# Loads and position products at the start of a hybrid S5 / pool / conformer step: small loads first, raw parameters turned in pairs, one product per position row

## The reference

```python
lam_bar = jnp.exp(lam * dt)
b_bar = ((lam_bar - 1.0) / lam)[..., None] * bmat
mod = jax.nn.silu(c) @ ada_w + ada_b
xs = x_sample + _grid_pos_embed(rows, GRID_W, D_MODEL)
h = _rmsnorm(x, norm1_g) * (1.0 + sc1) + sh1
z = h @ w_in
```

## Time and profile before

| | us |
|---|---|
| median of 3 runs | 1314.56 |
| lowest and highest run | 1313.19, 1315.68 |
| the profiled execution's own time | 1311.89 |
| its span, first to last instruction | 1310.0 |
| TensorE busy (share of the span) | 1219.5 (93%) |
| VectorE busy | 857.4 (65%) |
| ScalarE busy | 510.2 (39%) |
| POOL busy | 521.7 (40%) |

### The profile page before, as it was taken

The page is one execution under the profiler, slowest core; times in us unless marked ns, Lnnn a source line. Parts: engine busy times, 40 slices in busy tenths (PEclk is TensorE's granted clock), DMA queues, the critical chain, the costliest instruction groups (busy, mean ns, idle before and its releaser), DMA issues.

```text
span 1310.0 us, 21433 instructions
## 1 busy us (share of the span) xinstructions
PE 1219.5 (93%) x7574; PEld 1072.3 (82%) x7574; DVE 857.4 (65%) x1336; ACT 510.2 (39%) x911; POOL 521.7 (40%) x362
## 2 busy tenths in 40 slices
PE   3888899996699999899999999999999999999996
PEld 2478898786446888899999999999889999999995
DVE  2647959989944337667767666766855555555558
ACT  1464451126245547533333433433432333333223
POOL 0179425554343003455444445444533333333330
PEclk9889999997799999999999999999999999999998
DMA  8833345389872333766666576566677778777781
GB/s 273 313 110 120 114 140 177 102 109 229 270 290 97 104 121 102 252 226 229 219 208 211 189 256 224 213 219 220 237 232 250 240 260 277 255 249 264 242 279 73
DMA packets 189569, 268.52 MB, mean 205 GB/s; under 512 B 14030, under 2 KB 108536, under 8 KB 186824
## 3 DMA queue, kind: packets, MB, share of 16 engines
q1 hardware_dynamic: 187952, 263.00, 61.8%
q0 software_dynamic: 1280, 4.72, 0.9%
q10 hardware_dynamic: 280, 0.09, 0.0%
HBM read 186.49 MB, written 81.26 MB: 204 GB/s over the span
## 4 chain that ended last, share of the span: by engine, by line
PE 79%; DVE 8%; ACT 3%; DMA 3%; issue 3%; POOL 2%; SPq 1%; ACTq 0%; DVEq 0%; POOLq 0%
PE banks L891 22%; PE banks L893 22%; PE banks L892 22%; PE banks L1163 3%; PE banks L927 1%; PE banks L1042 1%; PE banks L976 1%; DMA dn<-in_ssm_d 1%; POOL sst L820 1%; PE banks L1059 1%; PE banks L1065 1%; PE banks L962 1%; ACT nts L1700 1%; DVE dsel L1959 1%; PE banks L935 1%
## 5 line engine op out<-in xcount | busy, mean ns | idle before, releaser
L843 POOL TENSOR_TENSOR raw13r<-raw13s,w13h 128x512 fp32r<-128x512 f32 x110 | 155.4, 1421 | 467.0 <-ACT w13h L1652 421.8
L892 PE MATMUL banks<-ntr,w13h 128*128 128x256 f32 (+1 forms) x1144 | 336.8, 294 | 0.0
L891 PE MATMUL banks<-ntr,w13h 128*128 128x256 f32 (+1 forms) x968 | 283.0, 292 | 3.4 <-POOL raw13r L843 2.2
L892 PEld LDWEIGHTS banks<-ntr,w13h 128*128 128x128 f32 x1144 | 215.9, 189 | 0.9
L891 PEld LDWEIGHTS banks<-ntr,w13h 128*128 128x128 f32 x968 | 183.0, 189 | 5.6 <-issue 2.5
L891 PE MATMUL banks<-f2h,f_hi 128*128 128x512 f32 x396 | 156.7, 396 | 0.4 <-DVE acc L2360 0.4
L893 PE MATMUL banks<-f2h,f_lo 128*128 128x512 f32 x396 | 156.2, 395 | 0.0
L892 PE MATMUL banks<-f2l,f_hi 128*128 128x512 f32 x396 | 156.2, 395 | 0.0
L893 PE MATMUL banks<-ntr,raw13r 128*128 128x256 f32 (+1 forms) x528 | 153.9, 291 | 0.0
L2226 DVE TENSOR_TENSOR acc<-acc,banks 128x512 f32<-128x512 f32 x170 | 112.9, 684 | 38.9 <-PE banks L893 30.8
L847 POOL TENSOR_TENSOR f2l<-f2s,f2h 128x1024 fp32r<-128x1024 f32 x44 | 106.3, 2437 | 34.7 <-ACT f2h L1656 34.7
(11 more groups left out here) (323 smaller groups left out, 2536.5 us busy)
## 6 DMA issues: line engine op xcount, KB each, us to landing
raw13s<-in_ffn_w SPq DMA_DIRECT2D x66, 512.0 KB, 4.5
parts<-w13h SPq DMA_DIRECT2D x110, 256.0 KB, 2.5
w13h<-parts SPq DMA_DIRECT2D x110, 256.0 KB, 2.8
f2s<-in_ffn_w SPq DMA_DIRECT2D x44, 512.0 KB, 4.2
ad<-in_ada_w SPq DMA_DIRECT2D x20, 1024.0 KB, 9.1
parts<-wsumr SPq DMA_DIRECT2D x66, 256.0 KB, 2.6
wsumr<-parts SPq DMA_DIRECT2D x55, 256.0 KB, 4.9
parts<-raw13r SPq DMA_DIRECT2D x44, 256.0 KB, 2.9
```

What stands on the lines that cost most here:

```text
L843: nc.gpsimd.tensor_tensor(w13_low(x, f), w13_low(x, f, F32), w13h[x][:, :, :].bitcast(F32), ALU.subtract).then_inc(sem("w13_lo"), 1)
L891: nc.tensor.matmul(out, hi_w, hi_x, start=start, stop=False)
L892: nc.tensor.matmul(out, hi_w, lo_x, start=False, stop=False)
```

## The change

Seven edits, all before the first input projection:

- SP issues the two state rows, the taps and ssm_d, which ACT issued, behind the lambda rows, ahead of all large loads; ACT issues the nine groups of parameter rows alone.
- The four raw tensors lie on four quarters (32 partitions each) of one buffer, in a place of their own behind the eight modulation tiles.
- SP no longer waits for the raw turns; x tiles and modulation tiles 0 to 3 alternate.
- `raws_turn` turns two tensors at once: 16 transposes of 64 partitions for B, 32 products of 64 partitions for C. It signals twice instead of four times, and the readers' views go over two banks.
- POOL copies the identity into two selectors, `col_sel` (64 x 128) and `row_sel` (16 x 8 x 128).
- `pos_columns` and `pos_row` are one product each, of 128 output partitions, with these selectors.
- Position rows 4 and 5 go between the modulation tiles, rows 6 and 7 behind the eighth turn of x.

```diff
-    raw = [at(f"raw{i}", [32, 2 * HD * NS], O_NT + 40960 + i * 8192) for i in range(4)]
+    raw = at("raw", [4 * Q, 2 * HD * NS], O_NT + KT * 8192)
+    row_sel = at("row_sel", [16, 8, P], O_W2 + 4096)
+    col_sel = at("col_sel", [GRID_W, P], O_W2 + 8192)
...
-        for i, name in enumerate(("ssm_lam_re", "ssm_lam_im")):
+        for i, name in enumerate(("ssm_lam_re", "ssm_lam_im", "state_ssm_re", "state_ssm_im")):
             sp.dma_start(rlam[:, i, :], dview(A[name], 0, [[P, Q], [1, P]])).then_inc(sem("vectors_in"), 16)
-        ada_in(0)
-        ada_in(1)
+        sp.dma_start(rtap[:, :], dview(A["conv_dw_w"], 0, [[P, 2 * TAPS], [1, P]])).then_inc(sem("vectors_in"), 16)
+        sp.dma_start(dn[:, :], dview(A["ssm_d"], 0, [[32, NPAIR], [1, 32]])).then_inc(sem("vectors_in"), 16)
         for i, name in enumerate(("ssm_b_re", "ssm_b_im", "ssm_c_re", "ssm_c_im")):
-            sp.dma_start(raw[i][:, :], dview(A[name], 0, [[2048, Q], [1, 2048]])).then_inc(sem("raws_in"), 16)
+            sp.dma_start(raw[Q * i:Q * i + Q, :], dview(A[name], 0, [[2048, Q], [1, 2048]])).then_inc(sem("raws_in"), 16)
         sp.dma_start(pos_c[:, :], A["pos_cols"]).then_inc(sem("pos_in"), 16)
         sp.dma_start(pos_r[:, :], A["pos_rows"]).then_inc(sem("pos_in"), 16)
-        x_in(0)
-        ada_in(2)
-        x_in(1)
-        ada_in(3)
-        x_in(2)
-        x_in(3)
+        for n in range(4):
+            x_in(n)
+            ada_in(n)
         ada_in(4)
         ada_bias(0)
-        sp.wait_ge(sem("raws_turned"), 3)
         for n in range(5, KT):
             ada_in(n)
...
+        pool.wait_ge(sem("ident"), 1)
+        nc.gpsimd.tensor_copy(view(col_sel, 0, [[GRID_W, 2], [1, GRID_W]], 0, GRID_W),
+                              view(ident, 0, [[0, 2], [1, GRID_W]], 0, GRID_W)).then_inc(sem("ident"), 1)
+        nc.gpsimd.tensor_copy(view(row_sel, 0, [[GRID_W, 16], [1, GRID_W]], 0, 16),
+                              view(ident, 0, [[1, 16], [0, GRID_W]], 0, 16)).then_inc(sem("ident"), 1)
...
-            for i in range(4):
-                for h in range(HD):
-                    if i < 2:
-                        last = tr(B[i][:, h * Q:(h + 1) * Q], view(raw[i], h, [[HD, P]], 0, Q), ident[0:Q, 0:Q])
-                    else:
-                        for par in range(2):
-                            c0 = par * HD * NS + h * NS
-                            last = mm(B[i][64 * par:64 * par + 64, h * Q:(h + 1) * Q], raw[i][:, c0:c0 + NS], ident[0:Q, 0:Q], start=True, stop=True)
-                last.then_inc(sem("raws_turned"), 1)
+            turn = [ident[2 * Q * i:2 * Q * i + 2 * Q, 2 * Q * i:2 * Q * i + 2 * Q] for i in range(2)]
+            for h in range(HD):
+                last = tr(view(banks, 2 * Q * h, [[1, 2 * Q]]), view(raw, h, [[HD, P]], 0, 2 * Q), turn[0])
+            last.then_inc(sem("raws_turned"), 1)
+            for h in range(HD):
+                for par in range(2):
+                    c0 = par * HD * NS + h * NS
+                    last = mm(view(banks, 1024 + 2 * Q * h, [[1, 2 * Q]], 64 * par, 64), raw[2 * Q:4 * Q, c0:c0 + NS], turn[1], start=True, stop=True)
+            last.then_inc(sem("raws_turned"), 1)
...
-            for e in range(2):
-                mm(B[7][64 * e:64 * e + 64, :], ident[0:GRID_W, 0:GRID_W], pos_c[:, :], start=True, stop=True)
+            pe.wait_ge(sem("ident"), 3)
+            mm(B[7][:, :], col_sel[:, :], pos_c[:, :], start=True, stop=True)
...
-            for e in range(2):
-                last = mm(B[5 + i % 2][64 * e:64 * e + 64, :], ident[0:16, 2 * i + e:2 * i + e + 1].broadcast_to([16, GRID_W]), pos_r[:, :], start=True, stop=True)
-            last.then_inc(sem("pos_bank"), 1)
+            mm(B[5 + i % 2][:, :], row_sel[:, i, :], pos_r[:, :], start=True, stop=True).then_inc(sem("pos_bank"), 1)
...
-        ada_tiles(0, 4, KT, B[4])
-        pos_row(4)
-        pos_row(5)
+        for k in range(4, KT):
+            ada_tiles(0, k, k + 1, B[4])
+            if k < 6:
+                pos_row(k)
         ada_bias_add(0, B[4])
         x_turns(0, 2)
         mod_turn(0, B[4])
-        x_turns(2, 4)
+        x_turns(2, 8)
         pos_row(6)
         pos_row(7)
-        x_turns(4, 8)
...
-        act.wait_ge(sem("raws_turned"), 3)
-        A_(view(cc, 0, [[1, HD], [HD, Q]]), B[2][:, :], ACT.Copy).then_inc(sem("cc_evac"), 1)
-        act.wait_ge(sem("raws_turned"), 4)
-        A_(view(cc, Q * HD, [[1, HD], [HD, Q]]), B[3][:, :], ACT.Copy, scale=-1.0).then_inc(sem("cc_evac"), 1)
+        act.wait_ge(sem("raws_turned"), 2)
+        for r in range(2):
+            A_(view(cc, r * Q * HD, [[1, HD], [HD, Q]]), view(banks, 1024 + Q * r, [[2 * Q, HD], [1, Q]]), ACT.Copy,
+               scale=-1.0 if r else 1.0).then_inc(sem("cc_evac"), 1)
...
-        dve.wait_ge(sem("raws_turned"), 2)
+        dve.wait_ge(sem("raws_turned"), 1)
-        bank = lambda b: B[b][:, :].rearrange("p (h q) -> p h q", q=Q)
+        bank = lambda r: view(banks, Q * r, [[2 * Q, HD], [1, Q]])
```

More of the change, by code:

```diff
@@ L1328, in _ @@
             act.dma_start(dst(), src()).then_inc(sem("vectors_in"), 16)
[L1329 to L1332, removed]
         act.wait_ge(sem("pv_evac"), 2)
@@ L1928, in _ @@
         dve.wait_ge(sem("ada_tile"), KT)
-        dve.wait_ge(sem("raws_turned"), 4)
+        dve.wait_ge(sem("raws_turned"), 2)
         def h_parts(n):
```

## The result

The changed kernel takes 1301.45 us (median of 4 runs, 1299.26 to 1303.85) against 1313.88 for the kernel before in the same series (1312.15 to 1315.68): a ratio of 0.9906, interval 0.9883 to 0.9928, so 12.4 us faster, give or take 3. The forecast was 1300.4. The profiled execution took 1301.54, its span 1299.7.

A forecast was written before the change was run, and what follows sets the result against it. The prediction followed the edited front, where TensorE waited until 20.7 us for the last small load. Bias 12.2 earlier plus 2.0 from the turns of x made 14.2: 1297.7 for this execution, 1300.4 as median, range 1293.5 to 1308.

The forecast's parts named there:

- Release of TensorE: Start of the kernel: the last small load lands at 6.5 us, so TensorE starts 14.2 earlier than at 20.7.
- the early bound: TensorE's release: last small load issued at 4.14 plus 1.8 to land, 5.9 us; the late bound was 11.
- VectorE's adds: VectorE's chain ahead of row 2 only moves; the first two position adds end at 30.3 us.
- One product per row saves nothing: Position rows on TensorE: half-width products already overlap, so one product costs the same 1.9 us; otherwise 0.95 saved a row.
- Raw turns: Paired turns on TensorE: transposes 1.8 us, 64 products 4.5 (3.5 to 7.0); TensorE ready at 27.8, ahead of VectorE's 30.3.
- Row 2 to the bias: Position rows and modulation tiles on TensorE: 14.9 us instead of 12.8, bounds 9.0 to 18.1; bias ends at 45.2, 12.2 earlier.
- Rows 6 and 7 behind the turns: Two position rows leave the middle of the eight turns of x: 2.0 us gained.
- my bound of 3.61: Turns of x: the most that taking out the two position rows could gain, the 3.61 us they stood there.
- No wait in SP's queue: Load issue on SP: last tile in at 38.2, w_in at 42.2, wanted at 45.8, so hidden by 3.6 us.
- What comes behind: From 107 us on POOL's pieces set the time, so the front's gain arrives whole; a POOL pause comes every 8.97.
- the two rivals that went by a whole period: VectorE ops waiting for POOL pauses: one missed, 5.2 us gained, 1309.3 (13%); or one won, 1291.4 (7%).
- The front has no cover: Chain up to 160 us: no slack seen; the rival, gain ending in a later wait, 1314.6, had 5%.

The follow-up runs named there:

- The run that had no lead at dsel: The changed kernel with the old order of loads, four small ones again on ACT and two modulation tiles ahead of the raw tensors: 1314.39 us, ratio 1.0007.
- the useless products: The changed kernel with the second pair of raw tensors turned twice into the same bank, 64 products more: 1294.99 us, ratio 0.9855.

## Why the prediction was right, and where it wasn't

The sum was right: 14.2 us forecast at the end of the front, 14.25 measured at dsel. Two of its terms were not, the bias by 2.6 one way and the turns by 2.6 the other; that they cancelled is luck.

- **Release of TensorE**: 6.11 for 6.5, 14.6 earlier. The last small load landed 2.37 after its issue, near the 1.8 of the earlier trace rows, so the early bound (5.9) was the better choice. The sentence on the Trainium skill ("DMA: Bandwidth & Descriptors", Queues, rings and completion order) put the release there too. With large loads ahead of the small ones, TensorE was released at 20.7 in the kernel before and at 20.2 in the run with the old order; for that case the pace stays as the earlier trace rows show it.
- **VectorE's adds**: end at 29.85 for 30.3.
- **One product per row saves nothing**: right, 2.07 at the 1.2 level; two halves 1.97.
- **Raw turns**: 5.6 for 6.3, in the bounds; the wider turns took the time of the narrow ones (64 in 3.68, the bound of 3.5). I read this as TensorE being ready earlier, at 27.3 for 27.8, and counted nothing for the wait that it leaves.
- **Row 2 to the bias** is the step that failed: 14.9 forecast, 17.9 measured, next to the upper bound of 18.1. I took 2.4 us for row 2 and tile 3, most of it at the 2.4 level, and let the clock come back after tile 6. It was at 1.2 from row 2 into tile 7: the pause had taken it before row 2, and it did not come back while rows and tiles alternated. That is 1.5 on row 2 and tile 3 (3.9 for 2.4) and 0.5 on tile 7. The other 1.0 is my prices: at the 1.2 level a row takes 2.00 and a tile 1.87, not 1.85 and 1.7. The 24 in 4.8 of the earlier trace rows, which I read as one price, are a mix, as the clock came up at 42.79 in them. The bias ended 9.56 earlier, not 12.2.
- **Rows 6 and 7 behind the turns**: 2.0 forecast, 4.6 gained between the bias and POOL's start (14.19 less 9.56), above my bound of 3.61. The move itself was sized well, since putting the rows back costs 2.1 in the median and 1.5 in the trace. The rest goes with the clock: it was up for most of the turns (the last three took 1.0 to 1.2 each on TensorE, against 4.97/3 = 1.66 in the earlier trace rows). The bound had left out that the turns themselves could become faster.
- **No wait in SP's queue**: hidden, as said; with the wait back the time is the same.
- **What comes behind**: dsel again ended at POOL's pause. No pause of POOL was won or lost, here or in any run: from the start of the first projection to the end of dsel it was 45.9 to 46.1 in all fourteen traces. So the two rivals that went by a whole period, 20% of the chance together, didn't occur though that start lay anywhere from 57.9 to 78.3; POOL's work moved along with it (by 14.19 here).
- **The front has no cover** held for the median: 12.4 of 14.2, within the interval. In the trace, 14.25 at dsel became 10.36 at the end; part of that is the trace of before, which was itself 2.67 below its median, as the forecast had said. The run that had no lead at dsel lost 5.2 in the same stretch.

## What to carry to other kernels

When a path is shortened, look at who now waits where nobody waited: a stretch that is done early on TensorE opens a pause, and the pause can cost more than the stretch gave. So judge a TensorE saving ahead of a wait by the granted clock behind the wait. Small loads that gate the start go ahead of the bulk, in every queue: with the raw tensors moved ahead of the modulation tiles, that was the whole gain here.

## What the runs showed of the hardware

**A pause, and then half speed for 16 us.** In the eight traces with new loads in which TensorE waited 1.27 to 3.54 us before row 2, the clock fell to the 1.2 level before the start of row 2 or within 3.8 us behind it (in the latest case after a second pause, of 0.91); in the four that had no pause there it was at 2.4 through row 3 once it had come up. While single rows and single tiles alternated, it stayed where it was: at 1.2 in the changed kernel, though TensorE was busy without a break (0.50 from 30 to 46 us), and at 2.4 with the useless products. In a run of four or five tiles it came back. Ahead of tiles 0 to 2 the durations say 1.2 as well (rows 0 and 1 took 3.67 to 3.78 together): TensorE worked without a break from about 12 us, on rows, raw turns and tiles, and in these twelve traces the first clock entry, 1.00, came only at 25.0 to 32.6. The Trainium skill ("TensorE: Matmul & The Clock Gate", HAM oscillation — how this bites in real kernels) tells of the same trap, groups of matmuls between waits, each starting slow; the traces agree on the fall, and show besides that a busy engine can stay slow. What in the alternation keeps the clock from coming back was not tried.

**The same pause can cost nothing.** Late in the kernel TensorE waits 3.02 us for VectorE, in both kernels. TensorE's timeline of the changed kernel there, then of the kernel before:

```profile
922.91 0.41 PE L895 MATMUL banks<-extr,w13h 128*128 128x320 f32 x1 [3.02 <-DVE u L2184]
```

```profile
934.80 0.41 PE L891 MATMUL banks<-extr,w13h 128*128 128x320 f32 x1 [3.02 <-DVE u L2186]
```

The windows behind the wait, again the changed kernel and then the kernel before:

```profile
922.00:926.00 4.00, 3.09 (x14) 3.10 (x15) 3.25 (x7) 0.47 (x1) 0.00 (x0) 0.70 0.81 310
```

```profile
934.00:938.00 4.00, 3.20 (x22) 3.21 (x23) 3.83 (x8) 0.47 (x1) 0.00 (x0) 1.00 0.80 306
```

The clock fell in the one and not in the other, at the price of 1.5 us. Across this place the lead over the kernel before shrank by 1.4 to 2.6 us in nine of the thirteen later traces and by nothing in four. So a difference of 2 us between two single traces may be this alone; the runs don't show what decides it.

**More columns at no price.** 64 products that turn 64 columns each took 3.68, 128 that turn 32 took 7.04 in the run with the load order alone: 0.058 and 0.055 per product.
